# Three weight chunks held for block 1 instead of block 7, with the last stage reordered in halves

## The chip, the cores and the metric

The kernel runs on one core of one Trainium2 chip. The metric is the device time of one execution in microseconds. Five engines run beside each other and meet only at semaphores: TensorE (PE, matrix products, weight loads shown as PEld), VectorE (DVE), ScalarE (ACT), GpSimd (POOL) and SyncE (SP, which issues nearly all DMAs). All DMAs of the core share 16 DMA engines.

## The reference, cut to what matters

One layer of a decoder over 544 tokens (512 of a prompt, 32 of eight samples), all in float32:

```python
h = h + mixer(rmsnorm(h, g_mix))                   # projections, short conv, windowed attention, w_out
m = rmsnorm(h, g_ffn)
top_v, top_i = top_k(m @ w_router + b_router, 4)   # 4 of 32 experts for each token
for each block (rows of one expert e):
    u = (xb @ w_up[e] + b_up[e]).reshape(rows, 1024, 2)
    act = min(u0, 7) * sigmoid(1.702 * min(u0, 7)) * (clip(u1, -7, 7) + 1)
    y = act @ w_down[e] + b_down[e]
h = h + sum_k softmax(top_v)_k * y_k
gate = sigmoid(rmsnorm(h, g_ple) @ w_ple_gate)     # w_ple_gate is 1024 x 1024
h = h + gate * (p @ w_ple)
out = rmsnorm(h, g_final)
```

Of an expert, `w_up` holds 8 MB and `w_down` 4 MB; each is read once.

## The kernel before

**Stages.** From 0 to some 388 us: mixer, router, and the tables that say which rows go to which block. From 388 to 1408 us: the expert blocks, numbered 0 to 31 here (`nb` is 32). From 1408 us to the end, the last stage: the last rows of the experts are added in, then the gate product, the norms and the outputs, in five tiles of rows.

**A block.** Its weights are 12 chunks of 1 MB: eight of `w_up` (chunks 0 to 7), four of `w_down` (8 to 11). They lie in a ring of 12 places, `raw[0]` to `raw[11]`, one for each chunk number, taken in six pairs `raw2[q]`. `body(i)` on PE multiplies the eight up chunks of block i and then the four down chunks of block i - 1. Blocks 2 and 3 (`SMALL`) take two groups of rows instead of three, so PE spends less on each of their chunks, and the chunks are no smaller.

**Who asks for weights, and when.** SP's `body(i, first)` runs one block ahead. For pair q it waits at `tiles_done` until PE has finished both chunks of this pair in the block before, and then issues one 2 MB DMA into the place that has come free. So a pair is asked for two chunks after the block's start plus two for each pair before it, and is needed when PE reaches the same place a block later. SP issues in the order of the code; a wait holds all that is written behind it.

**The stash.** Beside the ring lie three more places, `ahead[0]`, `ahead[1]` (together `ahead2`) and `ahead[2]`. With `STASH = 7` they are filled at 388 us with chunks 0 to 2 of block 7. When SP comes to block 7 it skips pair 0 and asks only for chunk 3 of pair 1. PE reads these three chunks from `ahead`.

**The last stage.** `w_ple_gate` comes as four quarters, `gate_r[0]` to `gate_r[3]`. `gate_r[0]` has a place of its own and is asked for behind block 8; the others go into ring places that come free in the last body. For each, ACT makes `gate_h` (`round_ple`) and DVE `gate_l` (`split_ple`), so that PE can multiply in three passes: `gate_h` by `nTh`, `gate_l` by `nTh`, `gate_h` by `nTl` (L2028 to L2030). DVE runs `split_ple(2)` and `split_ple(3)` ahead of `yn` and `yl`, which take the last block's rows out of PSUM; ACT runs `round_ple(2)` and `round_ple(3)` ahead of `yh`. PE's `last_rows` needs `yh` and `yl`, then come 14 products whose result nobody reads (`FILL`, L2698), and then tile 0: DVE adds four planes of expert rows to `hq[0]` (`add_rows`, L1906), adds PSUM (`h_rows`, L1934), multiplies by the gain `gple` into `xnb` (L1937, L1946), PE transposes `xnb` (`n_turn`, L2646), ACT and DVE make `nTh` and `nTl`, and PE runs the four quarters (`gates_of`). `n_turn(1)` stands before the last quarter of tile 0.

Of the kernel before, what the change touches and what calls it, by code (L numbers as in the profile page):

```python
# [13 lines left out]
F32 = mybir.dt.float32  # L14
# [3 lines left out]
ALU = mybir.AluOpType  # L18
# [3 lines left out]
P = 128  # L22
# [54 lines left out]
STASH = 7  # L77
# [14 lines left out]
FILL = 14  # L92
X_SLOT = [0, 1, 2, 2, 3]
# [3 lines left out]
def build(nc, A, O):  # L97

    with ExitStack() as ctx:
# [161 lines left out]
        gple = at("gple", [P, D], F32, R0 + 26848)  # L261
        gpl4 = at("gpl4", [P, QD], F32, R0 + 33120)
# [202 lines left out]
        nrow_half = sem("nrow_half")  # L465
# [3 lines left out]
        nrow = sem("nrow")  # L469
# [37 lines left out]
        def _(sp):  # L507
# [118 lines left out]
            for c in (0, 1):  # L626
                sp.dma_start(raw[UPC + c][:], one(w_dn, 0, c)).then_inc(landed[UPC + c], 16)
            sp.wait_ge(pp_mm, NT)
            sp.dma_start(raw[3][:], one(w_up, 0, 3)).then_inc(landed[3], 16)
            sp.wait_ge(b_rnd, 2)  # L630
            sp.wait_ge(tab_done, 1)
            e_ahead = sp.value_load(tabE[0:1, STASH:STASH + 1], min_val=0, max_val=NEXP - 1)
            sp.dma_start(ahead2[:], w_up[bass.ds(e_ahead, 1), 0].rearrange("e p n -> (e p) n")).then_inc(ahead_in, 16)
            sp.dma_start(ahead[2][:], one(w_up, bass.ds(e_ahead, 1), 2)).then_inc(ahead_in, 16)
# [9 lines left out]
            def body(i, first):  # L644
# [6 lines left out]
                stash = isinstance(i, int) and i == STASH  # L651
                for q in range((UPC if first else BLK) // 2):
                    l = 2 * q
                    if stash and q == 0:
                        continue
                    sp.wait_ge(tiles_done, TB + l + 2 if first else TB + 12 * i - 16 + l + 2)
                    if stash and q == 1:
                        sp.dma_start(raw[3][:], one(w_up, bass.ds(e_cur, 1), 3)).then_inc(landed[3], 16)
                        continue
                    if first:  # L660
                        src = w_up[1, q]
# [12 lines left out]
            with sp.Fori(PEEL, STASH) as i:  # L674
                body(i, False)
            body(STASH, False)
            body(STASH + 1, False)
            sp.dma_start(gate_r[0][:], A["w_ple_chunks"][1]).then_inc(ple_in, 16)
            with sp.Fori(STASH + 2, end) as i:
                body(i, False)  # L680
            e_prev = sp.value_load(tabE[0:1, bass.ds(nb - 1, 1)], min_val=0, max_val=NEXP - 1)


            sp.wait_ge(xh_done, nb)
            for g in range(3):
                sp.dma_start(bd3[NEXP * g:NEXP * g + NEXP].bitcast(F32), bs_dram[:, g % 2, 2 * FF:]).then_inc(bd_in, 16)
            sp.dma_start(gple[:], A["g_ple_rows"]).then_inc(gf_in, 16)
            for l in range(DNC):
                sp.wait_ge(tiles_done, TB + 12 * nb - 16 + l + 1)
                sp.dma_start(raw[l][:], one(w_dn, bass.ds(e_prev, 1), l)).then_inc(landed[l], 16)  # L690
# [4 lines left out]
            sp.wait_ge(tiles_done, TB + 12 * nb - 7)  # L695
# [560 lines left out]
        def _(dve):  # L1256
# [636 lines left out]
            def add_rows(i):  # L1893
# [3 lines left out]
                for k in range(0, TOPK, 1 if i == 0 else 2):  # L1897
# [4 lines left out]
                    elif k == 2:  # L1902
                        dve.wait_ge(y_in, 16)
# [908 lines left out]
```

## Time and profile before

| | us |
|---|---|
| median of 3 runs | 1496.08 |
| the runs | 1495.47 to 1502.73 |
| the profiled execution: its time | 1496.07 |
| the profiled execution: span from the first to the last instruction | 1494.2 |
| PE busy | 1463.3 (98% of the span) |
| DVE, ACT, POOL busy | 733.3, 246.4, 99.4 |
| moved by DMA | 492.14 MB, mean 329 GB/s |

The stages are read by the chain that ended last and by the table of stretches; the rows used are given word for word below. A DMA's row gives the time from its issue to its landing. "Issued at" is read from SP's rows.

### The profile page before, as it was taken

How to read it: one execution, taken by the hardware profiler on the slowest of the kernel's cores; microseconds unless marked ns; L12 is line 12 of the kernel's file. 1: busy time of each engine (PE TensorE's matmuls, PEld its weight loads, DVE VectorE, ACT ScalarE, POOL GpSimd, SP SyncE). 2: the span in 40 equal slices, each digit the busy share in tenths (PEclk: the TensorE clock that was granted, in tenths of full speed). 3: DMA queues.
4: the chain of work that ended last, by engine and by line, in shares of the span. 5: the costliest groups of instructions: out<-in, count | busy, mean ns of one | idle time of the engine just before them, and what ended most of it. 6: DMA issues, size and time to landing. Idle time of an engine off the chain costs nothing.

```text
span 1494.2 us, 36367 instructions
## 1 busy us (share of the span) xinstructions
PE 1463.3 (98%) x15688; PEld 816.3 (55%) x15688; DVE 733.3 (49%) x1643; ACT 246.4 (16%) x449; POOL 99.4 (7%) x130
## 2 busy tenths in 40 slices
PE   9999999999999999999999999999999999999987
PEld 8999999987543334333344333344333344333575
DVE  5468333354655444543354543354543454545685
ACT  5433322224100000000000000000000000001236
POOL 0000000000000001000001000001000001000050
PEclk9999999999999999999999999999999999999999
DMA  8421922356999999999999999999999999999861
GB/s 285 146 63 52 324 87 86 110 190 246 342 375 405 413 414 413 404 410 416 415 414 415 405 407 415 414 415 412 401 410 411 413 412 411 399 408 411 342 215 47
DMA packets 57305, 492.14 MB, mean 329 GB/s; under 512 B 11079, under 2 KB 16439, under 8 KB 27300
## 3 DMA queue, kind: packets, MB, share of 16 engines
q1 hardware_dynamic: 50212, 473.59, 79.7%
q0 software_dynamic: 6928, 17.49, 3.3%
q8 instruction: 53, 0.87, 0.2%
q14 instruction: 16, 0.13, 0.0%
q10 hardware_dynamic: 96, 0.07, 0.0%
HBM read 478.28 MB, written 29.53 MB: 340 GB/s over the span
## 4 chain that ended last, share of the span: by engine, by line
PE 89%; DVE 4%; DMA 3%; ACT 2%; issue 1%; SPq 0%; DVEq 0%; ACTq 0%
PE ps L2494 41%; PE ps L2504 21%; PE ps L2088 11%; PE ps L2279 3%; DMA raw_pair<-w_up_pairs 3%; PE ps L2028 2%; PE ps L2030 2%; PE ps L2029 2%; PE ps L2491 2%; PE ps L2473 1%; ACT S L900 1%; DVE hq L1906 1%; DVE S L1316 1%; PE ps L2310 0%; PE ps L2659 0%
## 5 line engine op out<-in xcount | busy, mean ns | idle before, releaser
L2494 PE MATMUL ps<-raw_pair,xT 128*32 128x512 f32 x5688 | 620.6, 596 | 0.0
L2494 PEld LDWEIGHTS ps<-raw_pair,xT 128*32 128x32 f32 x5688 | 182.6, 111 | 422.3 <-issue 422.3
L2504 PE MATMUL ps<-raw_pair,acT 128*32 128x256 f32 x5760 | 316.3, 379 | 0.0
L2504 PEld LDWEIGHTS ps<-raw_pair,acT 128*32 128x32 f32 x5760 | 187.1, 110 | 135.9 <-issue 17.4
L1790 DVE TENSOR_SCALAR gl<-ps 128x256 f32<-128x256 f32 x94 | 34.2, 419 | 438.0 <-ACT gl L1094 438.0
L1832 DVE STREAM_TRANSPOSE acT<-arow 32x192 f32<-32x192 f32 (+1 forms) x512 | 187.1, 366 | 7.4
L1822 DVE STREAM_TRANSPOSE xT<-xg 32x256 f32<-32x256 f32 x372 | 161.8, 435 | 11.5 <-DMA xg<-m_rows,ius 5.8
L1094 ACT ACTIVATE gl<-ps 128x256 f32<-128x256 f32 x94 | 29.4, 384 | 651.2 <-PE ps L2494 623.9
L2088 PE MATMUL ps<-aTh,wh 128*128 128x272 f32 x512 | 107.3, 291 | 0.1
L2088 PE MATMUL ps<-aTh,wl 128*128 128x272 f32 x512 | 106.0, 289 | 0.0
L2088 PE MATMUL ps<-aTl,wh 128*128 128x272 f32 x512 | 105.7, 288 | 0.0
L1260 DVE TENSOR_TENSOR wl<-raw_pair,wh 128x2048 fp32r<-128x2048 f32 x21 | 48.1, 2291 | 80.7 <-ACT wh L820 80.7
L2088 PEld LDWEIGHTS ps<-aTh,wh 128*128 128x128 f32 x512 | 80.4, 189 | 1.0 <-issue 0.4
L2088 PEld LDWEIGHTS ps<-aTl,wh 128*128 128x128 f32 x512 | 80.5, 189 | 0.0
L2088 PEld LDWEIGHTS ps<-aTh,wl 128*128 128x128 f32 x512 | 80.1, 189 | 0.0
L1811 DVE TENSOR_SCALAR yrow<-ps,gside 32x256 f32<-32x256 f32 x87 | 42.6, 490 | 69.5 <-PE ps L2504 68.7
L1103 ACT ACTIVATE yrow<-ps,gcol 96x768 f32<-96x768 f32 x29 | 26.0, 897 | 274.3 <-PE ps L2504 274.3
L750 POOL DMA_INDIRECT xg<-m_rows,iug x26 | 25.8, 991 | 378.5 <-DMA m_rows<-mrow 354.3
L820 ACT ACTIVATE wh<-raw_pair 128x2048 fp32r<-128x2048 f32 x21 | 40.2, 1912 | 20.7 <-PE ps L2088 11.4
L755 POOL COPY iug<-rowi 128x1 uint32 x25 | 8.3, 330 | 461.9 <-DVE xT L1822 461.9
L761 POOL DMA_INDIRECT y_rows<-yrow,ius x27 | 25.6, 946 | 197.4 <-issue 197.4
L1797 DVE SCALAR_TENSOR_TENSOR arow<-gl 128x256 f32<-128x256 f32 x94 | 34.4, 421 | 1.0
(436 smaller groups left out, 1215.0 us busy)
## 6 DMA issues: line engine op xcount, KB each, us to landing
raw_pair<-w_up_pairs SPq DMA_DIRECT2D x122, 2048.0 KB, 16.0
raw_pair<-w_down_pairs SPq DMA_DIRECT2D x60, 2048.0 KB, 17.1
raw_pair<-w_mix SPq DMA_DIRECT2D x25, 1024.0 KB, 5.2
raw_pair<-w_up_pairs SPq DMA_DIRECT2D x9, 1024.0 KB, 5.4
y_rows<-c_zero SPq DMA_DIRECT2D x4, 2176.0 KB, 21.6
raw_pair<-w_down_pairs SPq DMA_DIRECT2D x8, 1024.0 KB, 19.0
yk<-y_rows SPq DMA_DIRECT2D x8, 1024.0 KB, 8.4
raw_pair<-w_ple_chunks SPq DMA_DIRECT2D x4, 1024.0 KB, 21.9
```

The costliest lines, as they stand in the source:

```text
L820: nc.scalar.activation(wh[slot][:], raw[s][:], ACT.Copy).then_inc(rounded, 1)
L1260: nc.vector.tensor_tensor(wl[slot][:], raw[s][:], wh[slot][:].bitcast(F32), ALU.subtract)\
L1790: nc.vector.tensor_scalar(gl[:, 1, b, :], src, LIMIT + 1.0, 1.0 - LIMIT, ALU.min, ALU.max)\
L1797: nc.vector.scalar_tensor_tensor(out=arow[:, LB * b:LB * b + LB], in0=gl[:, 0, b, :], scalar=SILU_MAX, in1=gl[:, 1, b, :], op0=ALU.min, op ...
L1811: ins = nc.vector.tensor_scalar(yrow[32 * g:32 * g + 32, SETS * LB:], ps[CAP:P, 3 + g, 0:LB], gside[CAP:P, g, bass.ds(b, 1)], None, ALU.mult)
L1822: ins = nc.vector.transpose(dst[32 * r:32 * r + 32, :, 32 * g:32 * g + 32], xg[32 * g:32 * g + 32, :].rearrange("p (k n) -> p k n", n=P)[: ...
L1832: ins = nc.vector.transpose(dst[32 * r:32 * r + 32, 0:nk, 32 * g:32 * g + 32], arow[32 * g:32 * g + 32, 0:P * nk].rearrange("p (k n) -> p ...
L2028: mmul(out, ah, bh, start=first, stop=False)
L2088: ins = mmul(out[:, 512 * b:512 * b + HALF], w, a[:, k, HALF * b:HALF * b + HALF], start=(k == 0 and a is aTh and w is lh), stop=(k == KT ...
L2279: ins = mmul(out[:, 512 * b:512 * b + HALF], w, y[:, CT * r + k, HALF * b:HALF * b + HALF], start=(k == 0 and w is lh and y is yTh), stop= ...
L2494: ins = mmul(ps[32 * j:32 * j + 32, b, :], xT[:, k, 32 * g:32 * g + 32], w[:, 512 * q:512 * q + 512], start=False, stop=(k == UPC - 1))
L2504: ins = mmul(ps[32 * j:32 * j + 32, bank + b, 0:LB], a, raw[slot][:, D * (k % 2) + LB * q:D * (k % 2) + LB * q + LB], start=(k == 0), stop ...
```

## The change

There are two parts.

**The weights.** `STASH` is 1. `ahead[1]` is asked for once the router's products are done, `ahead[0]` behind `raw[3]` of block 0, `ahead[2]` once the tables are there. In the requests for block 1, pair 0's place takes pair 0 of block 2, pair 1's takes chunk 3 of block 1 alone, and pairs 2 and 3 are as before. Block 2's requests skip pair 0. Block 7 is a block like the others. `gate_r[0]`, and a new table `gpc` of 4 KB, are asked for behind block 5 (the code's `PEEL` is 6).

**The last stage.** The gain `g_ple` goes into the gate weights instead of the rows: `round_ple` and `split_ple` scale by a column of `gpc`, in four pieces of 512 columns each, so `gple`, `gpl4` and the products into `xnb` are gone and PE transposes `hq` itself. The quarters are stored in another order, by rows of the weight first. The last block's `w_down` chunks are asked for ahead of `bd3`; `gple` (512 KB) is no longer loaded; `gate_r[3]` is asked for behind the rows of tile 0. Tile 0 is added, turned and split in two halves of its columns; `n_turn(1)` stands behind the last quarter of tile 0 instead of before it, with `FILL1` = 5 unread products behind it.

```diff
-STASH = 7
+STASH = 1
+FILL1 = 5
# SP, ahead of the bodies
+            sp.wait_ge(b_rnd, 2)
+            sp.wait_ge(lg_mm, NT)
+            sp.dma_start(ahead[1], one(w_up, STASH, 1)).then_inc(ahead_in, 16)
             sp.wait_ge(pp_mm, NT)
             sp.dma_start(raw[3][:], one(w_up, 0, 3)).then_inc(landed[3], 16)
-            sp.wait_ge(b_rnd, 2)
+            sp.dma_start(ahead[0], one(w_up, STASH, 0)).then_inc(ahead_in, 16)
             sp.wait_ge(tab_done, 1)
-            sp.dma_start(ahead2[:], w_up[bass.ds(e_ahead, 1), 0].rearrange("e p n -> (e p) n")).then_inc(ahead_in, 16)
-            sp.dma_start(ahead[2][:], one(w_up, bass.ds(e_ahead, 1), 2)).then_inc(ahead_in, 16)
+            sp.dma_start(ahead[2][:], one(w_up, STASH, 2)).then_inc(ahead_in, 16)
# SP, body
-                    if stash and q == 0:
+                    if isinstance(i, int) and i == STASH + 1 and q == 0:
                         continue
                     sp.wait_ge(tiles_done, TB + l + 2 if first else TB + 12 * i - 16 + l + 2)
-                    if stash and q == 1:
-                        sp.dma_start(raw[3][:], one(w_up, bass.ds(e_cur, 1), 3)).then_inc(landed[3], 16)
+                    if first and q == 1:
+                        sp.dma_start(raw[3][:], one(w_up, STASH, 3)).then_inc(landed[3], 16)
                         continue
-                    if first:
-                        src = w_up[1, q]
+                    if first and q == 0:
+                        src = w_up[bass.ds(expert_of(STASH + 1), 1), 0].rearrange("e p n -> (e p) n")
+                    elif first:
+                        src = w_up[STASH, q]
# SP, the end
+            for l in range(DNC):
+                sp.wait_ge(tiles_done, TB + 12 * nb - 16 + l + 1)
+                sp.dma_start(raw[l][:], one(w_dn, bass.ds(e_prev, 1), l)).then_inc(landed[l], 16)
             sp.wait_ge(xh_done, nb)
             for g in range(3):
                 sp.dma_start(bd3[NEXP * g:NEXP * g + NEXP].bitcast(F32), bs_dram[:, g % 2, 2 * FF:]).then_inc(bd_in, 16)
-            sp.dma_start(gple[:], A["g_ple_rows"]).then_inc(gf_in, 16)
# ACT, round_ple; DVE's split_ple has the same four pieces, with
# scalar_tensor_tensor(gate_r * gpc - gate_h)
-                nc.scalar.activation(gate_h[g - 1][:], gate_r[g - 1][:], ACT.Copy).then_inc(rounded, 1)
+                for j in range(KH):
+                    cols, k = slice(512 * j, 512 * j + 512), KH * ((g - 1) // 2) + j
+                    ins = nc.scalar.activation(gate_h[g - 1][:, cols], gate_r[g - 1][:, cols], ACT.Copy, scale=gpc[:, k:k + 1])
# PE
-                body(i, False)
+                body(i, False, True)
...
+            def n_turn_half(hf):
+                pe.wait_ge(h_add if hf else h_half, 1)
+                for k in range(4 * hf, 4 * hf + 4):
+                    ins = nc.tensor.transpose(slot2(2)[:, P * k:P * k + P], hq[0][:, P * k:P * k + P], ident[:])
+                ins.then_inc(ntr, 1)
...
+                    if i == 0 and g == 0:
+                        n_turn_half(1)
-                    if g == (1 if i else 2) and i + 1 < NT:
+                    if at_g == (1 if i else 3) and i + 1 < NT:
+                        if i == 0:
+                            bias_rows(2)
+                            last_rows(2)
                         n_turn(i + 1)
```

SP's queue from `raw[3]` of block 0 to block 2's up pairs, before. `raw_pair_49` to `raw_pair_52` are the pairs 0 to 3 of the ring:

```order
L629 DMA raw_pair_50<-w_up_pairs 128x2048
...
L633 DMA ahead_pair<-w_up_pairs 128x4096
L634 ISA
L634 DMA ahead_last<-w_up_pairs 128x2048
L636 DMA bsel2f<-c_bsel 8x256
L649 DMA bup<-bias_parts 4x512 x2
L666 DMA raw_pair_49<-w_up_pairs 128x4096
L666 DMA raw_pair_50<-w_up_pairs 128x4096
L666 DMA raw_pair_51<-w_up_pairs 128x4096
L666 DMA raw_pair_52<-w_up_pairs 128x4096
...
L666 DMA raw_pair_49<-w_up_pairs 128x4096
```

And the same place now:

```order
L628 DMA ahead_pair<-w_up_pairs 128x2048
L630 DMA raw_pair_50<-w_up_pairs 128x2048
L631 DMA ahead_pair<-w_up_pairs 128x2048
L633 DMA ahead_last<-w_up_pairs 128x2048
...
L666 DMA raw_pair_49<-w_up_pairs 128x4096
L656 DMA raw_pair_50<-w_up_pairs 128x2048
L666 DMA raw_pair_51<-w_up_pairs 128x4096
L666 DMA raw_pair_52<-w_up_pairs 128x4096
...
L648 DMA bup<-bias_parts 4x512
L666 ISA
L666 DMA raw_pair_50<-w_up_pairs 128x4096
```

One of the three chunks has moved ahead of `raw[3]`, the four requests for block 1 bring 7 MB instead of 8, and block 2's first request (`raw_pair_49`) is gone from its place behind them.

DVE's queue from `split_ple(2)` to tile 0's first split, before:

```order
L1873 TENSOR_TENSOR gate_l_205<-raw_pair_51,gate_h_209 128x2048
L1873 TENSOR_TENSOR gate_l_206<-raw_pair_51,gate_h_210 128x2048
L1909 REGISTER_ALU
L1911 TENSOR_SCALAR yn<-ps,gate_199 32x256 x3
...
L1906 TENSOR_TENSOR hq_179<-hq_179,yk_186 128x1024 x4
L1934 TENSOR_TENSOR hq_179<-ps,hq_179 128x512
L1937 TENSOR_TENSOR xnb<-hq_179,gple 128x512
L1934 TENSOR_TENSOR hq_179<-ps,hq_179 128x512
L1937 TENSOR_TENSOR xnb<-hq_179,gple 128x512
L1958 TENSOR_TENSOR nTl<-ps,nTh 128x512 x2
```

And now:

```order
L1877 SCALAR_TENSOR_TENSOR gate_l_204<-raw_pair_51,gpc,gate_h_208 128x512 x4
L1877 SCALAR_TENSOR_TENSOR gate_l_205<-raw_pair_51,gpc,gate_h_209 128x512 x4
L1927 REGISTER_ALU
L1929 TENSOR_SCALAR yn<-ps,gate_198 32x256 x3
...
L1916 TENSOR_TENSOR hq_179<-hq_179,yk_186 128x512 x6
L1924 TENSOR_TENSOR hq_179<-ps,hq_179 128x512
L1916 TENSOR_TENSOR hq_179<-hq_179,yk_186 128x512 x2
L1963 TENSOR_TENSOR nTl<-ps,nTh 128x512
L1924 TENSOR_TENSOR hq_179<-ps,hq_179 128x512
```

The splits of the second and third quarter still stand ahead of `yn`; behind it tile 0's first half is finished before the second half's last two additions, and the gain's products are gone.

## Rows read from the trace of the kernel before

**Rows 1.** What PE waited for over the span: us in total, times, longest us.
```profile
PE ps L2491 <- DMA raw_pair<-w_up_pairs: 3.8, 2, 2.6
...
PE ps L2628 <- DVE yl L1916: 3.3, 1, 3.3
```

**Rows 2.** Stretches: us, engines' busy us, granted clock, DMA share, GB/s.
```profile
418.00:427.00 9.00, 9.00 (x88) 2.74 (x84) 7.17 (x20) 0.00 (x0) 0.96 (x1) 1.00 0.92 340
...
497.00:531.00 34.00, 31.42 (x326) 11.64 (x324) 15.06 (x41) 1.62 (x4) 2.55 (x3) 0.92 1.01 413
...
597.00:629.00 32.00, 32.00 (x391) 12.88 (x387) 14.79 (x37) 1.83 (x4) 2.44 (x4) 1.00 1.01 410
...
1413.20:1420.10 6.90, 6.90 (x17) 5.36 (x17) 6.26 (x8) 0.80 (x1) 0.00 (x0) 0.51 1.02 417
```

**Rows 3.** The chain that ended last: start us, us, what.
```profile
597.99 20.74 PE ps L2494 x192
...
1397.50 10.54 PE ps L2504 x192
...
1462.33 0.23 PE ps L2029
...
1478.87 6.98 PE ps L2659 x128
```

**Rows 4.** SP's timeline, 386 to 440 us: start, us, line, DMAs.
```profile
395.20 15.78 SPq L666 DMA_DIRECT2D raw_pair<-w_up_pairs  x4
...
421.61 15.78 SPq L666 DMA_DIRECT2D raw_pair<-w_up_pairs  x4
```

**Rows 5.** DMAs issued at 410.7, 421.6, 426.8: KB, us from issue to landing.
```profile
raw_pair<-w_up_pairs SPq DMA_DIRECT2D x1, 2048.0 KB, 13.1
...
raw_pair<-w_up_pairs SPq DMA_DIRECT2D x1, 2048.0 KB, 7.7
...
raw_pair<-w_up_pairs SPq DMA_DIRECT2D x1, 2048.0 KB, 9.0
```

**Rows 6.** The same of DMAs issued at 564.9, 576.7 and 635.5.
```profile
raw_pair<-w_down_pairs SPq DMA_DIRECT2D x1, 2048.0 KB, 22.9
...
raw_pair<-w_up_pairs SPq DMA_DIRECT2D x1, 1024.0 KB, 13.6
...
raw_pair<-w_up_pairs SPq DMA_DIRECT2D x1, 2048.0 KB, 16.9
```

**Rows 7.** The same of DMAs issued at 1333.0, 1365.0 and 1381.3.
```profile
raw_pair<-w_down_pairs SPq DMA_DIRECT2D x1, 2048.0 KB, 21.0
...
raw_pair<-w_down_pairs SPq DMA_DIRECT2D x1, 2048.0 KB, 22.5
...
raw_pair<-w_ple_chunks SPq DMA_DIRECT2D x1, 1024.0 KB, 24.6
```

**Rows 8.** ACT's timeline in the last stage: start, us, instruction, [idle before].
```profile
1405.97 1.91 ACT L1143 ACTIVATE gate_h<-raw_pair 128x2048 fp32r<-128x2048 f32 x1 [0.98 <-DMA raw_pair<-w_ple_chunks]
...
1422.00 1.08 ACT L1209 ACTIVATE nTh<-ps 128x512 fp32r<-128x512 f32 x2 [8.01 <-PE ps L2646]
```

**Rows 9.** DVE's timeline there.
```profile
1407.92 2.29 DVE L1873 TENSOR_TENSOR gate_l<-raw_pair,gate_h 128x2048 fp32r<-128x2048 f32 x1 [0.60 <-ACT gate_h L1143]
1410.24 1.50 DVE L1911 TENSOR_SCALAR yn<-ps,gate 32x256 f32<-32x256 f32 x3
...
1412.84 0.41 DVE L1923 TENSOR_TENSOR yl<-yn,yh 96x256 fp32r<-96x256 f32 x1
...
1452.92 1.42 DVE L1995 SCALAR_TENSOR_TENSOR hq<-hq,rinvt,gfin 128x512 f32<-128x512 f32 x2
```

**Rows 10.** PE's timeline there.
```profile
1416.45 5.07 PE L2698 MATMUL ps<-bd,gT 96*128 96x512 f32 x14
...
1423.47 0.47 PE L2028 MATMUL ps<-gate_h,nTh 128*128 128x512 f32 x1 [1.07 <-DVE nTl L1958]
...
1435.21 1.09 PE L2646 MATMUL ps<-ident,xnb 128*128 128x128 f32 x8 [3.33 <-DVE xnb L1946]
```

## What the change does to the time: the prediction

> **What bounds the kernel now.** I read the chain of work that ended last first, then the table of stretches, what PE waited for, and the DMA issues one by one with their times to landing. The chain is PE nearly throughout. In the long middle a normal block has 192 up products in 20.74 us, so 2.6 us for each of its eight up chunks [rows 3], as much for each down chunk (192 products in 10.54 us, the last four, which end at 1408.0), and 0.9 for the biases: 32.0 us a block, with PE busy for all of the 32 us from 597 to 629 [rows 2]. But the DMA engines are full beside it: share 1.01 at 410 GB/s [rows 2]. Twelve chunks of 1 MB in 32 us are 393 GB/s before any row is gathered or scattered. So two resources have nearly the same price per block, and what keeps PE fed is the head start of the weights.
>
> That head start is read as a latency. Pair 0 is asked for 0.9 + 2 x 2.6 = 6.1 us into a block and needed at the start of the next, 25.9 us later; every other pair has 26.8. A request in a full queue waits for all in front of it. The latency is 22.9 us for a request at 564.9, falls to 13.6 at 576.7, right where block 7's three chunks are skipped, is 16.9 at 635.5 and creeps to 21.0 at 1333.0 and 22.5 at 1365.0 [rows 6, 7]. Only around blocks 2 to 5, whose small blocks use weights faster than they come, does PE wait for them: 3.8 us [rows 1], and the mean granted clock of 497 to 531 is 0.92 [rows 2], so part of it ran at 1.2 instead of 2.4 GHz.
>
> In the last stage three waits stand in PE's way: 3.3 us for `yl` [rows 1], 1.1 for tile 0's `nTl` and 3.3 for tile 1's `xnb` [rows 10].
>
> **The change, part by part.**
>
> *The early chunks.* The purpose could only be reached if the weights of blocks 2 to 5 landed earlier. Before, block 1's four pairs are asked for from 395.2 on and block 2's from 421.6 on [rows 4], each when its ring place comes free. The pair asked for at 421.6 landed in 7.7 us, against 13.1 for the one at 410.7 [rows 5]: the queue had just run empty, and the DMA share from 418 to 427 is 0.92 [rows 2]. So all that the stash of block 7 cost in front had been worked off by then. Now block 2's pair 0 comes with the early requests, and 4 MB fewer are in the queue by 421.6 (three of the stash, one loaded while the queue was idle before 388). But the next request, block 2's pair 1, still waits for chunk 3 of block 1 and goes out at 426.8, as before. With 7 MB after 395 instead of 8 and 3 before it instead of 4, the queue is empty at about 418, and stands idle until 426.8. From there on every request is the one that was made before, at the same time. What is gained is at most the difference between the 9.0 us that this request took and the 7.7 of a request into an empty queue [rows 5]: 0 to 1.3 us; I take the middle, 0.65. The stalls of blocks 2 to 5 stay.
>
> *The Trainium skill on this.* The queue's full rate bears on how fast such a backlog melts: the trace moves 410 to 413 GB/s with all engines busy [rows 2]. The Trainium skill, "DMA: Bandwidth & Descriptors", section Specifications, gives a fabric ceiling of 435 GB/s and an HBM limit of some 358 GB/s for a core. By the second, 12 MB could not come in 32 us and PE would starve in every block, so the trace speaks against it; by the first, the backlog would melt (the second rival below).
>
> *Block 7's 3 MB come back into the full queue.* From 587.8 (564.9 + 22.9) to 590.3 (576.7 + 13.6) [rows 6] 1 MB landed: 2.5 us for each. Three are 7.5 us; I take 7.6 with the requests' own cost. All landings behind are later by 7.6 - 0.65 = 6.95 us, for as long as the queue is never empty, which it is not to the end: no latency falls to 7.7. The cover: at 635.5 the slack is 25.9 - 16.9 = 9.0, so nothing is seen there. `gate_r[0]` (2.5 us) moves from behind block 8 to behind block 5; the slack of 26.8 - 22.9 = 3.9 at 564.9 hides it. At 1333.0 the slack is 26.8 - 21.0 = 5.8, so PE has to wait for weights, 1.1 us by then; at 1365.0 it is 26.8 - 22.5 = 4.3 [rows 7], so 2.7 us in all. The last down product then ends at 1408.0 + 2.7 = 1410.7, and at up to 1414.1 if the clock halves for 6.8 us behind a wait (from 1413.2 to 1420.1, behind the wait for `yl`, it was 0.51) [rows 2].
>
> *The gate quarters.* The third one, `gate_r[2]`, was asked for at 1381.3 and landed at 1405.9 [rows 7]. It is 6.95 us later, less 1.3 for `gple` (512 KB, half of 2.5), which was in front of it: 1411.5. Then ACT rounds it, four pieces of 1.08 / 2 = 0.54 from a 512-column row, 2.1 us instead of 1.91 [rows 8]; DVE splits it, four pieces of 1.42 / 2 = 0.71 instead of 2.29, 2.85 us [rows 9]; done at 1416.5. `yn` is queued behind this on DVE, and `yh` behind the rounding on ACT. PE's end of the experts (1410.7 to 1414.1) is covered. `yn` starts at 1416.6 instead of 1410.24 [rows 9]: **+6.3 us**, and everything behind moves with it, because `last_rows` needs `yl`.
>
> *The halves.* From `yl` (1413.25) to tile 0's first gate product (1423.47) there were 10.2 us [rows 9, 10]: `last_rows`, FILL's 14 products in 5.07 at the low clock, transposes, ACT, DVE. DVE has the first half of `hq[0]` ready earlier than before (six half additions and one from PSUM, instead of four whole ones and two steps), but FILL stands in front on PE, so this buys nothing. The transposes of the second half are off the path, and the 1.07 wait with them, in exchange for the same ACT and DVE step for one half: **-0.3 us**. Behind it PE has the quarters in the order 0, 1, 2, 3 with the second half's transposes in between. `split_ple(4)` starts when ACT has rounded the quarter, 1.4 us after the first product, and takes 2.85 to 3.4, so `nTl`'s second half stands 5 to 5.5 us after it; PE wants it after 2 x 2.7 + 0.5 = 5.9. Tile 1's rows are done 9.3 to 12 us after the first product; PE wants them at 0.5 + 10.9 + 1.4 = 12.8. So the wait of 3.3 goes: **-3.3 us**. `gate_r[3]` lands some 10 us before it is used.
>
> *FILL1.* Five products of 0.23 [rows 3]: **+1.1 us** on PE's path; at the low clock twice that.
>
> *The rest.* The gain's products into `xnb` leave DVE, which makes it earlier, but PE has no wait there after tile 1. ACT's and DVE's extra pieces for the first two quarters lie beside the last body's products. `gpc` is 4 KB. Behind PE's last products (L2659, end 1485.9) nothing is changed: 8.3 us.
>
> *Sum against the profiled span:* 1494.2 + 6.3 - 0.3 - 3.3 + 1.1 = 1498.0, so +3.8 (+3.9 before rounding). The profiled execution's own time is 1496.07, as good as the median of 1496.08, so the median is forecast at **1500.0 us**.
>
> **The rivals.**
>
> 1. *The queue idles less than I say and the stalls of blocks 2 to 5 go.* Those are the 3.8 us of waits for up pairs [rows 1] and the time lost at the low clock, 0.08 x 34 = 2.7 from 497 to 531 [rows 2] and at most as much again behind it: 6.5 to 9.2 us. With the last stage's -2.5 and the late landings hidden by the same idle queue: 1484 to 1487. For it: 4 MB less are asked for by 421.6. Against it: the latency of 7.7 there. Chance 0.1.
>
> 2. *The backlog melts before the end.* If the queue gains 0.3 us a block on PE, as it did from 635 on (16.9 and falling), then over 24 blocks the 7 us are gone, the quarters land as before, and only the last stage is left: 1496.08 - 0.3 - 3.3 + 1.1 = 1493.6. Against it: the latency rises again to 21.0 at 1333.0 [rows 7]. Chance 0.15. The 435 GB/s of the Trainium skill's "DMA: Bandwidth & Descriptors", Specifications, would lead to this rival; the trace's 410 GB/s with full engines does not agree with it.
>
> 3. *The deeper queue costs more: slower than before by over 0.5%.* The queue is served at 32.0 us a block. If gathers and scatters, which share the engines, hold the weights up by 0.2 us more a block when 24 instead of 16 us of requests stand there, the quarters land 23 x 0.2 = 4.6 us later still: 1504.6. It decides from 0.16 us a block on. Against it: from 497 to 531, with the deep queue that still shows in the 22.9 us at 564.9, the rate was 413 GB/s, no less than later [rows 2, 6]. Chance 0.12.
>
> 4. *The change doesn't do what it says*, since block 1 must wait for all three chunks: the last is asked for at about 389 and block 1 begins at 415, so this costs nothing. Inside the forecast.
>
> **How the numbers follow.** The forecast (late quarters, 1500.0; 1496 to 1503.5 by the unknowns: 0 to 1.3 us of early gain, 0.1 us a block in the service, 0 to 1.7 of clock) has 0.63. The likeliest, so 1500.0 is predicted. The range reaches to rival 2 and to the beginning of rival 3: 1491 to 1505. About 0.5% is what a measurement of this kernel can tell from no change: below 1488.6 or above 1503.6. Faster: rival 1, 0.10. Slower: rival 3 and the forecast's upper edge, 0.15. Within: 0.75.
>
> **What the profile of the changed kernel would show.** The 3 us of waits of PE for up pairs around 495 and 530, still there; the DMA share from 418 to 427 well below 0.92; a latency of a request at about 635 of 24 us instead of 16.9; small waits of PE for `raw_pair` in the last five blocks; `gate_r[2]` landing near 1411 and `yn` behind it near 1416; no wait of 3.3 for tile 1. I am wrong if the waits of blocks 3 to 5 are gone, if the latency in mid-loop is below 20 us, or if `yn` starts with PE's last product rather than with `split_ple(3)`.

## The result, and the profile after

The changed kernel takes **1508.21 us** (median of 4 runs, 1505.31 to 1510.66) against 1496.86 us (1495.47 to 1502.73) for the kernel before beside it: ratio 1.0072, 95% interval 1.0054 to 1.0090. By this ratio it is slower by 10.8 us (8.1 to 13.5), where 3.9 were forecast, and it lies outside the range of 1491 to 1505. The profiled execution took 1507.6 us, with a span of 1505.7.

The stretches of the changed kernel, with the columns of [rows 2] (us, busy us of PE, PEld, DVE, ACT and POOL, granted clock, DMA share, GB/s):

```profile
384.00:388.00 4.00, 4.00 (x26) 2.86 (x24) 3.58 (x27) 1.02 (x1) 0.00 (x0) 1.00 1.02 385
418.00:427.00 9.00, 9.00 (x80) 3.56 (x83) 7.45 (x28) 0.00 (x0) 0.96 (x1) 1.00 0.44 173
497.00:531.00 34.00, 31.50 (x375) 11.89 (x371) 13.69 (x36) 1.62 (x4) 1.89 (x2) 1.00 1.01 412
600.00:632.00 32.00, 32.00 (x395) 12.87 (x391) 14.79 (x37) 1.83 (x4) 2.44 (x4) 1.00 1.01 415
...
1419.90:1430.10 10.20, 6.41 (x15) 5.07 (x16) 9.63 (x17) 0.42 (x1) 0.00 (x0) 0.50 1.02 418
```

The second line is the forecast's first point: from 418 to 427 the DMA engines stood idle more than half of the time (share 0.44, before 0.92 [rows 2]). The three chunks that are loaded early bought a pause of the queue, and not an earlier block 2. The first line is one that I hadn't read. This is the same stretch of the kernel before:

```profile
384.00:388.00 4.00, 4.00 (x26) 3.25 (x26) 3.53 (x28) 0.52 (x2) 0.00 (x0) 1.00 0.26 89
```

The queue was a quarter busy there. The idle time that `ahead[1]` fills is the time in which block 0's gather runs. The gather's issue (KB, us from issue to landing), first before, then after:

```profile
xg<-m_rows,iug POOLq DMA_INDIRECT x1, 5.5
```

```profile
xg<-m_rows,iug POOLq DMA_INDIRECT x1, 8.2
```

What PE waited for in the changed kernel (us in total, times, longest us), where [rows 1] had 3.8 and 3.3:

```profile
PE ps L2633 <- DVE yl L1934: 4.2, 1, 4.2
PE ps L2500 <- DMA raw_pair<-w_up_pairs: 4.0, 3, 1.6
...
PE ps L2633 <- ACT yh L1162: 3.9, 1, 3.9
...
PE ps L2492 <- DMA raw_pair<-w_down_pairs: 2.8, 2, 2.1
PE ps L2541 <- DMA xg<-m_rows,iug: 2.6, 1, 2.6
...
PE ps L2037 <- DVE nTl L1971: 1.7, 1, 1.7
...
PE ps L2503 <- DMA raw_pair<-w_up_pairs: 1.5, 3, 0.7
...
PE ps L2646 <- DVE hq L1952: 0.9, 1, 0.9
```

The stalls of blocks 3 to 5 (L2500) are still there, and a third one has come, at the start of block 6, where the kernel before had none:

```profile
567.32 0.95 PE L2500 MATMUL ps<-bup,bsel 8*128 8x512 f32 x3 [1.55 <-DMA raw_pair<-w_up_pairs]
```

The wait for `xg` is new. Of the small waits for `raw_pair` (L2503) only one stands in the last blocks (0.2 us at 1285); what these blocks lose shows in the chain and in their lengths, below. The wait of 3.3 us for tile 1's `xnb` is gone, but tile 2 now waits 1.7 us for `nTl`, where it had no wait before, and tile 3's transposes wait 0.9 for `hq` (before 0.3 for `xnb`).

The latencies, as in [rows 6, 7]: the request for weights at 638.9, and the one for `gate_r[2]` at 1387.7.

```profile
raw_pair<-w_up_pairs SPq DMA_DIRECT2D x1, 2048.0 KB, 23.8
```

```profile
raw_pair<-w_ple_chunks SPq DMA_DIRECT2D x1, 1024.0 KB, 28.0
```

23.8 us in mid-loop was forecast as 24 (before 16.9). In the last blocks the chain of work itself goes through the loads (start us, us, what); the last row is the second gate quarter, `gate_r[1]`. PE is no longer the only link:

```profile
1225.49 26.85 DMA raw_pair<-w_up_pairs
1257.94 27.11 DMA raw_pair<-w_up_pairs
1290.65 26.81 DMA raw_pair<-w_up_pairs
1323.06 26.89 DMA raw_pair<-w_up_pairs
...
1385.17 28.02 DMA raw_pair<-w_ple_chunks
```

The head start of a pair is 26.8 us, so each of the four pairs is just late. And the last stage on DVE, beside [rows 9] (start us, us, line, what, [idle before and its releaser]):

```profile
1415.94 5.39 DVE L1877 SCALAR_TENSOR_TENSOR gate_l<-raw_pair,gpc,gate_h 128x512 fp32r<-128x512 f32 x8 [11.05 <-ACT gate_h L1141]
1421.36 1.50 DVE L1929 TENSOR_SCALAR yn<-ps,gate 32x256 f32<-32x256 f32 x3
...
1423.95 0.41 DVE L1941 TENSOR_TENSOR yl<-yn,yh 96x256 fp32r<-96x256 f32 x1
```

`yn` starts at 1421.36 instead of 1410.24, 11.1 us later, right behind the split of the gate quarters, as the forecast said it would; 6.3 were forecast.

### The profile page after: what moved, and what is told of

Same layout as the page of the kernel before. It is cut to its first block, busy times and chain, and to the rows that moved or that the text cites. A ratio compares the mean times of both kernels' runs of the same rounds, so it can differ in the third digit from the quotient of the medians.

```text
span 1505.7 us, 36440 instructions
## 1 busy us (share of the span) xinstructions
PE 1463.0 (97%) x15693; PEld 822.6 (55%) x15693; DVE 730.0 (48%) x1654; ACT 248.7 (17%) x462; POOL 96.8 (6%) x130
## 4 chain that ended last, share of the span: by engine, by line
PE 77%; DMA 16%; DVE 4%; ACT 2%; issue 1%; SPq 0%; DVEq 0%; ACTq 0%; POOLq 0%
PE ps L2503 34%; PE ps L2513 16%; DMA raw_pair<-w_up_pairs 10%; PE ps L2097 10%; PE ps L2288 3%; PE ps L2037 2%; DMA raw_pair<-w_down_pairs 2%; PE ps L2039 2%; DMA raw_pair<-w_ple_chunks 2%; PE ps L2038 2%; PE ps L2482 1%; PE ps L2500 1%; ACT S L895 1%; DMA m_rows<-mrow 1%; DVE S L1318 1%
## 5 line engine op out<-in xcount | busy, mean ns | idle before, releaser
L2503 PE MATMUL ps<-raw_pair,xT 128*32 128x512 f32 x5688 | 618.5, 593 | 1.7 <-DMA raw_pair<-w_up_pairs 1.5
L2503 PEld LDWEIGHTS ps<-raw_pair,xT 128*32 128x32 f32 x5688 | 180.5, 110 | 423.8 <-issue 403.5
L2513 PEld LDWEIGHTS ps<-raw_pair,acT 128*32 128x32 f32 x5760 | 195.4, 110 | 129.8 <-issue 20.1
```

Of the source, the lines that this page charges most:

```text
L2503: ins = mmul(ps[32 * j:32 * j + 32, b, :], xT[:, k, 32 * g:32 * g + 32], w[:, 512 * q:512 * q + 512], start=False, stop=(k == UPC - 1))
L2513: ins = mmul(ps[32 * j:32 * j + 32, bank + b, 0:LB], a, raw[slot][:, D * (k % 2) + LB * q:D * (k % 2) + LB * q + LB], start=(k == 0), stop ...
```

## Adding it up from the trace

Read along the two traces, the 11.5 us between the spans lie here:

- Block 0's first product starts at 392.6 instead of 388.9: 3.7 us. Of these 2.6 are the wait for `xg`; 1.0 was already there at 368 us, ahead of the first changed request, and is the difference from one execution to the next.
- Between there and the last down product 2.7 us more: the four blocks from block 3 on take 124.8 us together (before 125.0; each block from its first bias product to the next block's), the middle ones 32.0 each in both, and blocks 24 to 30 take 32.2 to 32.6, 3.0 us more in all. PE's downs end at 1414.4 instead of 1408.0.
- `gate_r[2]` lands at 1415.8 instead of 1406.0, +9.8, and rounding and splitting it take longer than before, so `yn` is 11.1 later. Without the late start of 3.7 the landing is 6.1 later, where 5.65 were forecast (6.95 - 1.3).
- From `yn` to the last gate product there are 76.0 us; before there were 75.6. The 2.5 us that I had expected to gain in the last stage are not there in this trace. One trace can't settle a term of this size: in the five with the last stage as changed this stretch takes 74.0 to 78.7 us, in the four with the old one 75.1 to 76.6.

Two readings of this were in competition, and the forecast had counted neither of them. Either the bytes in the full queue cost more than the 7 us that I gave them, or the order of the start costs something by itself. The experiments below take the change apart.

## Experiments

All ratios are against the kernel before, timed beside each kernel on the same chip.

**The last stage alone.** The changed kernel, but with block 7's chunks in the three buffers, loaded as before:

```
-STASH = 1
+STASH = 7
-            sp.wait_ge(b_rnd, 2)
-            sp.wait_ge(lg_mm, NT)
-            sp.dma_start(ahead[1], one(w_up, STASH, 1)).then_inc(ahead_in, 16)
...
-            sp.dma_start(ahead[0], one(w_up, STASH, 0)).then_inc(ahead_in, 16)
+            e_ahead = sp.value_load(tabE[0:1, STASH:STASH + 1], ...)
+            sp.dma_start(ahead2[:], w_up[bass.ds(e_ahead, 1), 0]...).then_inc(ahead_in, 16)
...
```

> The changed kernel with the stash back at block 7 (requests, waits and the place of gate_r[0] as before), the last stage as changed. Late-quarters theory: the latency at about 635 us is 17 again, gate_r[2] lands near 1404 to 1405, yn starts near 1410, and the time is 1494 to 1498, no more than 1.5 above before. Rival, that the last stage itself costs the time: 1503 or more with yn still near 1410.

Measured: 1496.34 us, ratio 0.9985 (0.9972 to 0.9998). So the rest of the change doesn't cost anything; it brings 2.2 us (0.3 to 4.2) by the times. The 2.5 of the forecast lie inside; but up to 1.3 of the 2.2 may be the 512 KB of `gple` that are no longer loaded. The trace doesn't show a gain, but it is of the slowest of the ten runs (1499.26), which was 3.9 us late already at 368 us: a 2 MB load asked for at 641 us takes 19.4 us (before 16.7), `gate_r[2]` lands at 1406.5 and `yn` starts at 1411.9, all later than expected, and from `yn` to the last gate product it takes 77.1 us. What it shows is more waiting for `nTl` (before 1.1 [rows 10]), of it 2.3 us for the second half of tile 0:

```profile
PE ps L2639 <- DVE yl L1936: 4.0, 1, 4.0
...
PE ps L2039 <- DVE nTl L1965: 3.8, 2, 2.3
```

**The chunks alone.** The kernel before, with the change's loads and its block 1, and the old last stage:

```
-STASH = 7
+STASH = 1
+            sp.dma_start(ahead[1], one(w_up, STASH, 1)).then_inc(ahead_in, 16)
...
+                    if first and q == 1:
+                        sp.dma_start(raw[3][:], one(w_up, STASH, 3)).then_inc(landed[3], 16)
...
```

> The kernel before with the stash at block 1 alone, as the change has it (ahead[1] early, gate_r[0] behind block 5), the last stage as before. Late-quarters theory: block 0 starts 2.7 to 3.7 us late because its first gather waits behind ahead[1]; the latency at about 640 us is 24; gate_r[2] lands 9 to 11 us later than before, yn with it: 1506 to 1508.5. Rival (last stage at fault): 1500 or less.

Measured: 1505.94 us, ratio 1.0061 (1.0041 to 1.0080), 9.1 us slower, a little below the expected range. `gate_r[2]` lands at 1416.0 and `yn` starts at 1420.3, in step with the changed kernel. Nearly the whole loss is in the chunks. The two parts alone, 9.1 and -2.2, make 6.9 of the 10.8 us; the 3.9 between are within the intervals of the three ratios (4.4 us together).

**The early chunk asked for later.** The changed kernel, with `ahead[1]` behind block 0's own last piece, so that the gather has the queue to itself:

```
-            sp.wait_ge(b_rnd, 2)
-            sp.wait_ge(lg_mm, NT)
-            sp.dma_start(ahead[1], one(w_up, STASH, 1)).then_inc(ahead_in, 16)
             sp.wait_ge(pp_mm, NT)
             sp.dma_start(raw[3][:], one(w_up, 0, 3)).then_inc(landed[3], 16)
             sp.dma_start(ahead[0], one(w_up, STASH, 0)).then_inc(ahead_in, 16)
+            sp.wait_ge(b_rnd, 2)
+            sp.wait_ge(lg_mm, NT)
+            sp.dma_start(ahead[1], one(w_up, STASH, 1)).then_inc(ahead_in, 16)
```

> The changed kernel, ahead[1] asked for behind raw[3] and ahead[0] instead of ahead of them, so that the first gather has no 1 MB beside it. If the late start is that collision: the gather takes 5.5 us again instead of 8.2, the wait of 2.6 us for it is gone, and the time is 1504.5 to 1506. If the start was late for another reason: 1508.

Measured: 1502.62 us, ratio 1.0033 (1.0019 to 1.0047), lower than the expected 1504.5 to 1506. The gather's row is

```profile
xg<-m_rows,iug POOLq DMA_INDIRECT x1, 5.1
```

and block 0 starts at 389.4. `gate_r[2]` lands at 1411.0 (forecast 1411.5) and `yn` starts at 1416.4 (forecast 1416.6). With the collision taken away, the queue's part of the forecast's path stands. The downs end at 1410.7, and that this is the forecast's own number is luck. The forecast had PE starve by 2.7 us in the last blocks; here each of them takes 32.0 us. PE lost its time in blocks 5 and 6 instead (36.2 and 35.1 us), where waits for weights of 1.2 and 2.4 us were each followed by a stretch at a lower clock (mean granted clock 0.93 and 0.94; before 0.93 and 1.00, in the changed kernel 1.00 in both):

```profile
531.00:567.00 36.00, 33.64 (x383) 13.14 (x379) 15.58 (x40) 1.83 (x4) 1.49 (x3) 0.93 1.01 409
567.00:602.00 35.00, 35.00 (x403) 12.61 (x399) 12.60 (x32) 1.83 (x4) 2.45 (x4) 0.94 1.01 417
```

The profiled execution (1505.4) is also 2.8 us above this kernel's median.

**No chunk beside the ring at all.** The changed kernel without the three loads; block 1 takes its chunks from the ring like any other block:

```
-            sp.dma_start(ahead[1], one(w_up, STASH, 1)).then_inc(ahead_in, 16)
...
-            sp.dma_start(ahead[0], one(w_up, STASH, 0)).then_inc(ahead_in, 16)
...
-            sp.dma_start(ahead[2][:], one(w_up, STASH, 2)).then_inc(ahead_in, 16)
...
-                        up_chunk(l, xT1 if first else xT, ahead[l] if first and l < 3 else raw[l])
+                        up_chunk(l, xT1 if first else xT, raw[l])
...
```

> The changed kernel with no chunk held beside the ring at all: block 1's eight chunks come through the ring. Idle-queue theory: the three early chunks only leave the queue idle from 418 to 427, so taking them away costs no more than 1.5 us against the kernel with the late ahead[1] (1504 to 1507), and no collision with the gather. Rival, that the early chunks do give a head start of 3 MB: about 7 us slower than that kernel, 1511 or more.

Measured: 1504.08 us, ratio 1.0043 (1.0025 to 1.0060). Against the run before this one, the three chunks held for block 1 are worth 0.0010, or 1.5 us (the two intervals overlap, so anything from nothing to nearly 5 us). Held for block 7 they are worth 0.0058, or 8.7 us (5.5 to 11.8), by the two kernels with the new last stage. That is the core of the case: three buffers are worth what three chunks in a full queue cost only while the queue is full. Without them the queue has this stretch, with a share of 0.63 where the changed kernel has 0.44:

```profile
418.00:427.00 9.00, 9.00 (x85) 2.76 (x88) 8.56 (x30) 0.00 (x0) 0.96 (x1) 1.00 0.63 213
```

It, too, runs empty before block 2's requests come. The early load of 3 MB only makes the pause longer. In the kernel with the late chunk, whose block 0 starts as early as before, the same stretch shows it best:

```profile
418.00:427.00 9.00, 9.00 (x92) 2.73 (x84) 7.62 (x23) 0.00 (x0) 0.96 (x1) 1.00 0.14 44
```

**Another block for the three buffers.** The kernel of the last stage alone, with block 20 in place of block 7:

```
-STASH = 7
+STASH = 20
```

> The kernel of e1_tail_alone with the three buffers beside the ring holding block 20's chunks 0 to 2 instead of block 7's. Theory (the three chunks are worth 3 MB of a queue that is full from block 2 to the end, wherever the loop uses them, as long as the queue never runs empty for want of a free place; block 1 is the case where it runs empty): the same time as e1_tail_alone, 1495 to 1498, ratio 0.998 to 1.001, though the latency of a 2 MB load at 640 us is 23 to 25 us instead of 19.4, and falls by 7 us only behind block 20. Rival (block 7 is the right place, since blocks 2 to 6 run the backlog up and a relief there keeps TensorE from waiting): 1500 or more, ratio above 1.002, with waits of TensorE for raw_pair between 700 and 1000 us.

Measured: 1497.64 us, ratio 1.0011 (1.0000 to 1.0023). The median lies in the expected range, and the waits between 700 and 1000 us, which the rival wanted, are not there. But the ratio is just above its range, and its interval doesn't meet the one for block 7 (0.9985; 0.9972 to 0.9998): by the ratios block 20 is 3.9 us worse (1.3 to 6.5), and worth 4.8 us against no chunk where block 7 is worth 8.7. Where the 3.9 us lie is open, since the profiled execution (1493.69) was as much faster than its median. The latency was missed: 19.6 us at 642, not 23 to 25, and the rows of the requests at 642, 967 and 999 are

```profile
raw_pair<-w_up_pairs SPq DMA_DIRECT2D x1, 2048.0 KB, 19.6
```

```profile
raw_pair<-w_up_pairs SPq DMA_DIRECT2D x1, 2048.0 KB, 19.0
...
raw_pair<-w_up_pairs SPq DMA_DIRECT2D x1, 2048.0 KB, 11.5
```

The fall at the block with the held chunks, 19.0 to 11.5, is 7.5 us, three times the 2.5 that the forecast gave a megabyte. That the level before it is lower than I thought has, as I read it, two reasons. `gate_r[0]`, another megabyte, comes behind block 20 here (2.5 us less at 642), and PE waited longer for weights in blocks 3 to 5 (its two waits for up pairs are 3.9 us, in the kernel with block 7 2.5). A wait of PE should lower the latency by as much, since the queue works on while no place in the ring comes free; no run tests this. If it is so, the latency alone doesn't tell how late the landings are; the latency and PE's lag together do.

**Two megabytes more.** The kernel before, with two loads into buffers that block 7 has left:

```
             sp.dma_start(gate_r[0][:], A["w_ple_chunks"][1]).then_inc(ple_in, 16)
+            for d in (ahead[0], ahead[2][:]):
+                sp.dma_start(d, one(w_up, 0, 0)).then_inc(ahead_in, 16)
...
```

> The kernel before, with two more loads of 1 MB each (a chunk of w_up that nothing reads) asked for behind block 8, into the two buffers that block 7 has left; the write of the last stage's rows waits for them too, long after they are there. Theory (the end of the loop and the last stage's weights follow the bytes in the queue, 2.5 us for 1 MB): the latency at 640 us is 5 us above before's 16.9, about 22; gate_r[2] lands 5 us later, the downs end 2 to 5 us later, and the time is 1501 to 1502.5, ratio 1.003 to 1.004. Rival (the queue has slack, and what the changed kernel lost it lost by the order of block 1, not by bytes): within 1 us of before, ratio 1.000 to 1.001.

Measured: 1500.98 us, ratio 1.0040 (1.0023 to 1.0057), so 6.0 us for 2 MB, with 3.4 to 8.5 by the interval; 4.5 to 6 were expected. The request at 637.8 took

```profile
raw_pair<-w_up_pairs SPq DMA_DIRECT2D x1, 2048.0 KB, 24.8
```

7.9 us above the 16.9 of the kernel before, where 5 were expected; some of that is PE, which had lost less in this execution by then (blocks 3 to 6 took 121.1 us, before 125.0). For the same reason the downs end only 1.0 us later (1409.0), where 2 to 5 were expected, though the last blocks do wait for weights (32.5 to 32.6 us each). `gate_r[2]` lands at 1410.5, 4.5 us later, and `yn` 4.6. Bytes in the full queue are paid for at the end, at about 2.3 (by the landing) to 3 us (by the time) each megabyte.

**One early megabyte, and nothing else.** The kernel before, with one load at the change's first place, of data that nothing reads:

```
+            sp.wait_ge(b_rnd, 2)
+            sp.wait_ge(lg_mm, NT)
+            sp.dma_start(ahead[1], one(w_up, 0, 0)).then_inc(ahead_in, 16)
             sp.wait_ge(pp_mm, NT)
...
+            sp.wait_ge(ahead_in, 16)
             sp.dma_start(ahead2[:], w_up[bass.ds(e_ahead, 1), 0]...).then_inc(ahead_in, 16)
```

> The kernel before, with one more load of 1 MB (a chunk of w_up that nothing reads) asked for at the changed kernel's first place, behind the logits and ahead of block 0's last piece; block 7's pair of chunks waits for it on SyncE, since it goes to the same place. Theory (what an early load costs is the gather of block 0's rows, which shares the queue with it): the gather takes about 8 us instead of 5.55, TensorE waits 2.5 to 3.5 us more for xg, and the loop and the end come later by that: 1499 to 1500.5, ratio 1.0017 to 1.003. Rival (the loop is full from 430 us on, so a start that is 3 us later is caught up in the blocks before the ring runs dry): the gather is as slow, but the time within 1 us of before, ratio 0.9995 to 1.0008.

Measured: 1500.81 us, ratio 1.0022 (1.0009 to 1.0035), 3.3 us slower. The gather and PE's wait behind it:

```profile
xg<-m_rows,iug POOLq DMA_INDIRECT x1, 8.3
```

```profile
390.98 1.07 PE L2535 MATMUL ps<-ident,xg 96*128 96x96 f32 x8 [2.54 <-DMA xg<-m_rows,iug]
```

The time lies above the rival's range: the late start costs the kernel about what PE waited. The trace is less simple. This execution was 1.2 us late already at 368 us; behind the wait the clock was granted at half for 6.8 us from 391.5 on, and block 0 took 28.5 instead of 26.3 us. So block 1 starts 7.0 us later than before, and the downs end at 1412.0, 4.0 us later: blocks 3 to 6, where PE waits for weights, gave 3.0 us back (122.0 us against 125.0). The steady blocks gave nothing back; there PE has 32.0 us of work in a block and the queue as much. The clock wasn't low in the changed kernel's start (1.00 from 386 to 396), so part of the 3.3 may be the clock and not the wait.

**Moving the splits out of the way.** If `yn` waits for the split of quarters 2 and 3, the split can come later. The kernel with the late chunk, with rounding and splitting of quarters 2 and 3 behind `yn`, `yh` and `yl` and tile 0's first half:

```
-            split_ple(2)
-            split_ple(3)
...
             add_half(0, (2, 3))
             h_half_of(0)
+            split_ple(2)
+            split_ple(3)
...
```

> The kernel of e3_late_chunk with the work on the second and third gate quarter moved behind yn, yl and tile 0's first half, on DVE and on ACT. If the late quarters cost time because yn and yh are queued behind them: yn starts with PE's last down product, 4 to 5 us earlier against the landing of the quarters, and the time falls from 1502.6 to 1497.5 to 1500. If the time is lost elsewhere in the last stage: 1502 or more.

Measured: 1506.34 us, ratio 1.0060 (1.0039 to 1.0080), slower than without it. `yn` did start with PE's last product, and the gain was given back on DVE:

```profile
1409.17 1.50 DVE L1927 TENSOR_SCALAR yn<-ps,gate 32x256 f32<-32x256 f32 x3 [9.61 <-PE ps L2513]
...
1419.87 5.38 DVE L1877 SCALAR_TENSOR_TENSOR gate_l<-raw_pair,gpc,gate_h 128x512 fp32r<-128x512 f32 x8
1425.17 0.68 DVE L1962 TENSOR_TENSOR nTl<-ps,nTh 128x512 fp32r<-128x512 f32 x1
```

```profile
1426.00 0.77 PE L2037 MATMUL ps<-gate_h,nTh 128*128 128x512 f32 x1 [5.27 <-DVE nTl L1962]
```

5.4 us of splitting now stand between the rows of tile 0 and its `nTl`. The first gate product comes 13.8 us behind `yl`, instead of 9.5 in the kernel with the late chunk. Another 4 us are lost behind it, where tile 0's second half is 2.1 us late on PE. The same edit in the kernel of the last stage alone:

> The same move in the kernel of e1_tail_alone, where the quarters land before PE's last product. yn starts 2 us earlier, the gates' first product too: 1493.5 to 1495.5 against 1496.3. Rival: tile 2's rows, asked for once tile 0's eight additions are done and now 5 us later, hold tile 2 up: 1497 or more.

Measured: 1500.18 us, ratio 1.0018 (1.0006 to 1.0029), against 0.9985 without it. The rival's number held in both, but in the second not its mechanism: DVE adds tile 2's rows without a wait, and PE waits 3.4 us for tile 0's first `nTl` and 3.0 for its second half, both behind the split on DVE. Of the two places for the split the old one is the better; that DVE sets the pace here is read from these waits.

**The filling products.** Without the five behind tile 1's turn (`FILL1 = 0`), in the kernel of the last stage alone:

> The kernel of e1_tail_alone without the five unread products behind tile 1's transposes. If they lie on PE's path, 1.1 us less (1495.2). If PE waits there for nTl anyway, no change, or up to 1.7 us more where the clock falls to 1.2 GHz in the gap.

Measured: 1495.64 us, ratio 0.9977 (0.9959 to 0.9994). And with four instead of fourteen ahead of tile 0 (`FILL = 4`):

> The kernel of e1_tail_alone with 4 instead of 14 unread products ahead of tile 0. They take 3.6 us of PE at the low clock, and DVE has the first half ready 3.4 us before they end. If the clock comes back at the same time without them: 2.5 to 3.5 us less (1493 to 1494). Rival, that the clock stays at 1.2 GHz through the gap before tile 0: within 1 us of 1496.3 or above.

Measured: 1494.99 us, ratio 0.9986 (0.9972 to 1.0000). Both together:

> The kernel of e1_tail_alone (block 7's chunks held beside the ring, the new last stage) with four instead of 14 filling matmuls ahead of tile 0 and none behind tile 1's turn. The two apart gave 1494.99 and 1495.64 against 1496.34 for e1_tail_alone. Theory (the filling matmuls stand on TensorE's own path, and the clock that they hold up is worth less than they cost): the two add, 1492 to 1495, ratio 0.9965 to 0.998. Rival (without any filling the clock stays low longer through tiles 0 and 1, and the products pay for it): 1495.5 to 1498, ratio 0.999 to 1.001, with the low level after the first gate product for over 10 us in the row of the granted clock.

Measured: 1494.97 us, ratio 0.9986 (0.9976 to 0.9997), so they don't add. The three can't be told from 0.9985, and the 2.5 to 3.5 us expected of `FILL = 4` were not found. The stretch behind the wait for `yl` shows why, first with both taken away, then with `FILL = 4` alone:

```profile
1409.30:1423.00 13.70, 11.40 (x28) 8.30 (x29) 11.48 (x16) 3.43 (x6) 2.48 (x1) 0.50 1.03 416
```

```profile
1409.30:1423.00 13.70, 11.33 (x37) 8.40 (x38) 10.70 (x18) 3.68 (x7) 1.92 (x1) 0.75 1.02 416
```

Where PE had waited 4.0 us for `yl`, the clock was low for the whole 13.7 us, over tile 0's first gate products, which take 0.63 us each instead of 0.39. Where it had waited 1.7, half of it was low. By the times, what the filling costs and what the clock costs without it can't be told apart here. None of these is faster than the kernel of the last stage alone by a difference that the runs can tell.

## Why the prediction was wrong

**Right: the early chunks gain next to nothing.** The queue idles from 418 to 427 and the stalls of blocks 3 to 5 stay (four blocks in 124.8 us against 125.0). The forecast gave 0 to 1.3 us, the runs 1.5 with zero inside.

**Right: block 7's 3 MB come back, and are paid for at the end.** The latency of 23.8, the starved last blocks (2.7 us forecast, 3.0 found) and `yn` behind the split of the third quarter were all as written. The kernel with the late chunk confirms the queue's path, 1411.0 and 1416.4; its 1410.7 for PE's downs is luck, as said there. The price was perhaps a little low: 7.6 us for 3 MB; the times say 8.7 (5.5 to 11.8) for no chunk against block 7's, and 6.0 (3.4 to 8.5) for 2 MB.

**Missed: what the idle queue before 388 was for.** "One loaded while the queue was idle before 388" was the step that failed. The forecast counted this load as bytes gone from the later queue, and priced it at nothing. But POOL's gather of block 0's rows runs in just that time, on the same DMA engines, and PE waits for it. It took 8.2 us instead of 5.5, and all of the loop starts later. The one megabyte alone costs 3.3 us (1.3 to 5.2), and asking for it later in the changed kernel gives 5.8 back (2.4 to 9.2). The range for this was not even in the sum: of all the terms it was the only one for which I did not ask who else used the queue at that moment. None of the three signs of being wrong that the forecast named looks at the start of the loop, and none of them came.

**Missed: the last stage.** The wait of 3.3 for tile 1 went as forecast, and 0.4 us was lost from `yn` to the last gate product instead of 2.5 won. "PE has no wait there after tile 1" was the sentence that failed. A wait of 1.7 for tile 2 came in its place (1.9 to 3.0 in three of the four other traces with this last stage, none in that of the last stage alone), and one of 0.9 for tile 3. The wait for tile 0's first `nTl`, which the forecast took off the path, is 1.5 instead of 1.1. Behind the one for tile 2's `nTl` stand POOL's and DVE's rows:

```profile
1455.02 7.49 POOL L807 TENSOR_TENSOR yk<-yk 128x1024 f32<-128x1024 f32 x4 [8.64 <-DMA yk<-y_rows]
```

```profile
1457.99 2.77 DVE L2014 TENSOR_TENSOR hq<-hq,xnb 128x512 f32<-128x512 f32 x1
...
1475.13 0.69 DVE L2014 TENSOR_TENSOR hq<-hq,xnb 128x512 f32<-128x512 f32 x1
```

The same addition takes 2.77 us beside POOL's additions and 0.69 without them. POOL's additions for the next tile now fall on DVE's steps just ahead of tile 2's `nTl`. That this is what makes tile 2 late is read from the trace only; no run moved it. The times allow 0.3 to 4.2 us of gain for the last stage, so the forecast's 2.5 isn't refuted, only not found on the trace.

**Missed: what hides `gate_r[0]`.** The forecast moved it from behind block 8 to behind block 5 and wrote that the slack of 3.9 us hides it. In all five traces that have it behind block 5 PE waits 1.5 to 2.4 us for weights at the start of block 6, and in none of the nine others. No run moved it alone, and whether it costs time at the end is open: in the changed kernel the end of the chain goes through the landings of the gate quarters, not through PE. The kernel before is also a poor yardstick for blocks 3 to 6: its 125.0 us are the longest of the eight traces with block 7's chunks held (the other seven 121.1 to 122.5). With block 20's, block 1's or none they take 124.6 to 127.2.

**Small terms.** ACT's pieces are 0.63 us and not 0.54, DVE's 0.67 and not 0.71. From the third quarter's landing to `yn` it is 5.6 us, where 5.1 were forecast, and the eight pieces of two quarters are done in a row here (5.0 and 5.4 us), since the second lands 2.6 us ahead of the third. The clock was low for 10.2 us behind the wait for `yl`, not 6.8.

**The sum again, by the runs:** 3.3 for the early load, 8.7 for block 7's megabytes, -1.5 for the early chunks, -2.2 for the last stage with `gple` gone: 8.3 of 10.8 us. The forecast's terms for these were 0, 7.6, -0.65 and, with -1.3 for `gple` and +0.7 for the slower pieces, -3.1. The other 2.5 is the difference between what one early megabyte costs in the kernel before (3.3) and in the changed one (5.8). The interval of that difference (3.9 us to either side) is wider than itself, so it stays open.

**The rivals.** The third gave 1504.6 and was nearest, but by luck: its mechanism isn't there, the service of the deep queue is no slower (412 and 415 GB/s against 413 and 410). The second, that the backlog melts, is wrong in an instructive way. PE's 32.0 us a block and the queue's are so close that the latency neither melts nor grows by more than a few us over 24 blocks. The 358 GB/s for a core in "DMA: Bandwidth & Descriptors" of the Trainium skill, section Specifications, does not hold for the 412 and 415 GB/s of these stretches either.

## What to carry to other kernels

An idle DMA queue is not free time as long as a short transfer that somebody waits for runs in it. Before a load is moved to the front, look at which gather or small load runs in that stretch, and price its stretching; what stands behind it may be a loop that can't catch up. A buffer beside a ring is worth its bytes only where the queue is full between its load and its use, so hold the chunks for a block that comes after the queue has filled for good. Here block 7 was worth 8.7 us and block 20 4.8, so which such block it is may matter too; why stays open. Where two resources have the same price per step, a megabyte more is paid at the end, and of a late start only what the blocks with stalls give back is regained.

## What the runs showed of the hardware

- A gather of block 0's rows takes 5.1 to 5.5 us without the early load and 8.2 to 8.3 us with one load of 1 MB in front of and beside it. Its issue was 7 us behind the load's, and the load itself took

```profile
ahead_pair<-w_up_pairs SPq DMA_DIRECT2D x1, 1024.0 KB, 14.7
```

  with two megabytes of `w_down` ahead of it.
- Similar waits did not lead to the same clock. In the kernel before it was granted at 0.92 of full from 497 to 531 [rows 2], in the changed one at 1.00, with as much waiting in blocks 3 to 5. In the kernel with the late chunk it was 0.93 and 0.94 in the two stretches after that, up to 602 us. In the last stage the low stretch was 6.9 us in the kernel before, 10.2 in the changed one, and 13.7 in the one with the least filling.
